# Attention steps that open with all their small matmuls, and gate weights sent once, in a two-block transformer kernel on one core

## The chip, the core and the metric

The kernel runs on one core of a Trainium2 chip. The metric is the device time of one launch, in microseconds (us); the time before is the median of three runs. Five engines work side by side and meet through semaphores: PE (TensorE, the matmuls), ACT (ScalarE), DVE (VectorE), POOL (GpSimd) and SP (SyncE, which here only issues DMAs).

## The reference

Two transformer blocks run one after the other on a sequence of 512 tokens of width 1024; the first adds 16 meta tokens (so 528 columns). Cut to the parts that the change touches:

```python
# first block: u = rmsnorm(h); proj = u @ w_in, split into q_na, k_na, v_na, q_gl, k_gl, v_gl, g_gl, z_gl
o_na = neighbourhood_attention(q_na, k_na, v_na, rpb)   # 8 heads of 64, window 8 rows x 16 columns, and the meta tokens
la_f = log_sigmoid(z[..., :16] @ up_f + bias_f) / 16     # z_gl is 32 columns wide: 16 for each direction
la_b = log_sigmoid(z[..., 16:] @ up_b + bias_b) / 16
o_gl = gla_bidirectional(...)                            # gated linear attention, chunks of 64
h = h + rmsnorm(concat(o_na, o_gl) @ w_o) ; feed-forward with a convolution of width 3
# second block
q, k, v, qi, ki, wi, u, ga, gb = split(h @ w_in_2)
sel = top_k(sum_j wi_j * relu(qi_j . ki), 128)           # for each query, among the keys before it
s = q . k / 8 - slope * distance, over the selected keys ; p = softmax(s) ; out = p @ v
merged = sigmoid(ga) * (out @ w_attn_proj) + sigmoid(gb) * (conv(u) @ w_conv_proj) ; ...
```

## The kernel before

**Precision.** All data is float32. Every large product is made from halves rounded to the format that PE reads fast: a value x is hi(x) + lo(x), and hi·hi + lo·hi + hi·lo makes three matmuls of one (`product`). `uhi` and `ulo` are the halves of the first block's normed input, `xhi` and `xlo` those of the second's, `whi` and `wlo` those of a weight.

**Weights.** 226 units of 128 x 1024 (512 KB) come in the order in which PE uses them, by SP (`load_unit`), into a ring of four slots `raw`. ACT rounds each to `whi` (`hi_through`), then its low half `wlo` is made: by DVE for units 0 and 1 (`split_unit`), by POOL from unit 2 on. A semaphore `unit_split` counts the low halves, `unit_used` frees a slot.

**The order** is written by hand: each engine has its own function, in which its instructions stand in the order of execution. Nothing reorders them, so an engine that waits holds all that stands behind it.

**The start.** The unit of z (index 0) holds z's 32 columns four times, so that PSUM has z in four groups of 32 rows; the gates' second product (`gate_logits`) then takes hi and lo of z and of the up-projections in one matmul. PE warms up on a constant tile (`keep_running`), and then runs z (unit 0) and the first tile of q_gl (unit 1) together, k after k (`two_tiles`), each with three products; `ulo` of each k comes from DVE (`first_low`), which also adds the squares for the norm (`add_square`). The second q_gl tile follows in halves (`half_tile`, destination B).

**Neighbourhood attention.** A loop of 18 steps in PE's, ACT's and DVE's functions. In step st PE makes the scores of step st, the transposes of the softmaxed scores of step st-1 and the values of step st-2; scores lie in the PSUM banks of `B4` (called B), values in `G[:, 1]`. Between them stand *pieces*: quarters of the 16 mixed projection tiles (`piece`, 12 matmuls each, all in the bank pair `G[:, 0]`), with `NA_SHARE[st]` pieces for step st. A tile's first piece waits for the evacuation of the tile before it (`evac_done`), which DVE makes in `after_piece` after the tile's last piece. In step 13 the transposes also wait for `meta_s_read`, DVE's reading of the meta tokens' scores, and `values_by_token(3)` turns the last tile of vT.

**Second attention.** A loop of 19 steps of the same kind, with a softmax over up to 512 keys (`soft2` on DVE, `exp2` on ACT), selections by top-k on DVE in steps 0 to 7, and pieces of the gates' projections (`gate_piece`). The waits of the small matmuls are `s2_read` (scores: the banks have been read), `p2_done` (transposes: the exp is there), `pt2_done` (values: the transposed weights are copied), `rb_done` and `al_done` (each fourth step: the block before has been scaled and split). PE's order of a step before is

```python
if 1 <= st < 16: scores2(st)
for x in ps[0:2]: gate_piece(x)
if 1 <= st <= 16: transposes2(st - 1)
for x in ps[2:4]: gate_piece(x)
if 2 <= st <= 17: values2(st - 2)
if st >= 5 and st % 4 == 1: factors2(st // 4 - 1)
for x in ps[4:]: gate_piece(x)
```

with 4 or 5 pieces in the steps 0 to 7 and two in the steps 8 to 15.

## Time and profile before

| | |
|---|---|
| median of three runs | 1465.36 us (1464.08 to 1465.66) |
| the profiled execution: its time | 1464.7 us |
| its span | 1462.8 us |
| busy in it: PE, DVE, ACT, POOL | 1435.7, 808.8, 557.6, 540.6 us |
| start, to the first half tile of B | 0 to 21.8 us |
| neighbourhood attention | 147.5 to 260 us |
| second attention | 868 to 1000 us |

A row of an engine in order of time gives the start, the duration, the engine and line, the operation with its destination and sources, its shape, the number of instructions, and in brackets the idle time ahead of it with what ended it. Consecutive instructions of one kind can share a row. Matmuls overlap, so the end of a record can lie past the start of the next; the distance between two starts says what an instruction costs PE.

### The profile page before, as it was taken

The numbers are of one execution on the slowest core, as the hardware profiler recorded it, in microseconds if no ns is written. First come the engines' busy times: TensorE is split into PE (matmuls) and PEld (weight loads), VectorE is DVE, ScalarE is ACT, GpSimd is POOL, SyncE is SP. The second block draws the span as 40 slices with busy tenths as digits, with TensorE's granted clock in tenths as the row PEclk, the third lists the DMA queues.
The fourth block names the chain that finished last, engine by engine and source line by source line (L and its number), as shares of the span: only waits on it lengthen the run. The fifth ranks groups of instructions, "written<-read, shape, count | busy, mean of one in ns | idle before, by whom it ended". The sixth has DMA issues, their size and how long they took to land.

```text
span 1462.8 us, 21184 instructions
## 1 busy us (share of the span) xinstructions
PE 1435.7 (98%) x8908; PEld 1238.4 (85%) x8908; DVE 808.8 (55%) x1154; ACT 557.6 (38%) x879; POOL 540.6 (37%) x229
## 2 busy tenths in 40 slices
PE   9999999999999999999999999999999999999997
PEld 8989787999999999888788767678888888888887
DVE  6933545446666666455799789863353344332023
ACT  6532334453223233232522464455344333333221
POOL 3421111224434434444244323224434444544441
PEclk9999999999999999999999999999999999999999
DMA  7211221112322224886232212212223233323332
GB/s 256 92 48 43 71 71 44 58 58 89 100 87 98 90 88 152 296 283 233 87 100 92 87 58 87 73 44 87 88 85 129 101 130 111 130 90 101 102 114 87
DMA packets 44830, 155.16 MB, mean 106 GB/s; under 512 B 4992, under 2 KB 7680, under 8 KB 44736
## 3 DMA queue, kind: packets, MB, share of 16 engines
q1 hardware_dynamic: 44080, 151.19, 31.1%
q10 hardware_dynamic: 656, 2.62, 0.6%
q8 instruction: 71, 1.16, 0.3%
q14 instruction: 23, 0.19, 0.0%
HBM read 151.56 MB, written 2.10 MB: 105 GB/s over the span
## 4 chain that ended last, share of the span: by engine, by line
PE 76%; DVE 6%; ACT 1%; issue 1%; DVEq 0%; ACTq 0%
PE G L512 71%; DVE scb L2259 1%; DVE small L2257 1%; PE B L1069 1%; PE B L1093 1%; PE B L1041 1%; DVE G L1759 1%; PE G L1080 0%; PE B L482 0%; DVE xlo L1767 0%; DVE S L2310 0%; DVE B L2306 0%; PE G L783 0%; DVE G L2200 0%; DVE small L2313 0%
## 5 line engine op out<-in xcount | busy, mean ns | idle before, releaser
L437 POOL TENSOR_TENSOR wlo<-raw,whi 128x1024 fp32r<-128x1024 f32 x224 | 540.1, 2413 | 900.5 <-ACT whi L1185 900.4
L1185 ACT ACTIVATE whi<-raw 128x1024 fp32r<-128x1024 f32 x226 | 238.5, 1056 | 292.7 <-DMA raw<-wstream 182.3
L512 PE MATMUL G<-xhi,whi 128*128 128x512 f32 (+1 forms) x692 | 273.5, 395 | 2.0 <-DVE xlo L1767 1.8
L512 PE MATMUL G<-xhi,wlo 128*128 128x512 f32 (+1 forms) x692 | 267.3, 386 | 0.0
L512 PE MATMUL G<-xlo,whi 128*128 128x512 f32 (+1 forms) x692 | 267.0, 386 | 0.0
L512 PE MATMUL G<-uhi,whi 128*128 128x258 f32 (+2 forms) x1216 | 253.3, 288 | 8.2 <-DVE qna L1901 1.7
L512 PE MATMUL G<-ulo,whi 128*128 128x258 f32 (+2 forms) x1216 | 246.3, 283 | 0.0
L512 PE MATMUL G<-uhi,wlo 128*128 128x258 f32 (+2 forms) x1216 | 245.8, 282 | 0.0
L512 PEld LDWEIGHTS G<-uhi,whi 128*128 128x128 f32 x1216 | 187.9, 189 | 21.1 <-issue 14.5
L512 PEld LDWEIGHTS G<-ulo,whi 128*128 128x128 f32 x1216 | 188.2, 189 | 0.0
L512 PEld LDWEIGHTS G<-uhi,wlo 128*128 128x128 f32 x1216 | 188.1, 189 | 0.0
L512 PEld LDWEIGHTS G<-xhi,whi 128*128 128x128 f32 x692 | 129.9, 188 | 44.7 <-issue 15.0
L512 PEld LDWEIGHTS G<-xhi,wlo 128*128 128x128 f32 x692 | 129.9, 188 | 26.7
L512 PEld LDWEIGHTS G<-xlo,whi 128*128 128x128 f32 x692 | 130.0, 188 | 24.7
L512 PE MATMUL G<-yhi,whi 128*128 128x512 f32 (+1 forms) x396 | 145.4, 367 | 0.0
L512 PE MATMUL G<-yhi,wlo 128*128 128x512 f32 (+1 forms) x396 | 144.8, 366 | 0.0
L512 PE MATMUL G<-ylo,whi 128*128 128x512 f32 (+1 forms) x396 | 144.7, 365 | 0.0
L2132 DVE TENSOR_TENSOR yf<-tv,tg 128x512 f32<-128x512 f32 x22 | 27.9, 1268 | 130.3 <-ACT tg L1273 130.3
L512 PEld LDWEIGHTS G<-yhi,wlo 128*128 128x128 f32 x396 | 74.7, 189 | 12.1
L512 PEld LDWEIGHTS G<-ylo,whi 128*128 128x128 f32 x396 | 74.7, 189 | 12.0
L512 PEld LDWEIGHTS G<-yhi,whi 128*128 128x128 f32 x396 | 74.7, 189 | 12.0
L2231 DVE SCALAR_TENSOR_TENSOR B<-z,vec,B 128x512 f32<-128x512 f32 x116 | 80.0, 751 | 1.1
(342 smaller groups left out, 1669.9 us busy)
## 6 DMA issues: line engine op xcount, KB each, us to landing
raw<-wstream SPq DMA_DIRECT2D x226, 512.0 KB, 3.4
ada_in<-ada SPq DMA_DIRECT2D x40, 512.0 KB, 5.8
ada_late<-ada SPq DMA_DIRECT2D x8, 512.0 KB, 3.6
h<-hT SPq DMA_DIRECT2D x8, 264.0 KB, 3.8
out<-res SPq DMA_DIRECT2D x8, 256.0 KB, 2.5
biasn<-bias SPq DMA_DIRECT2D x2, 960.0 KB, 7.5
biasn<-bias ACTq DMA_DIRECT2D x2, 960.0 KB, 4.7
scan_keep<-scanm SPq DMA_DIRECT2D x1, 528.0 KB, 6.8
```

The costliest lines, as they stand in the source:

```text
L437: pool.tensor_tensor(wlo[:, i, :], raw[:, i, :], whi[:, i, :].bitcast(F32), ALU.subtract)\
L512: ins = pe.matmul(dst[:, x, 0:xw], w[:, slot, b * P:(b + 1) * P], u[:, k, off + x0:off + x0 + xw], start=(first and i == 0 and j == 0), st ...
L1041: pe.matmul(B4[:, e % 4, 0:P * (b + 1)], qi2[par * 64:(par + 1) * 64, j // 2, P * b:P * (b + 1)], ki2[par * 64:(par + 1) * 64, 0:P * (b + ...
L1069: last = pe.matmul(B4[:, par, 0:P * (b + 1)], q2[par * 64:(par + 1) * 64, m, P * b:P * (b + 1)], k2[par * 64:(par + 1) * 64, m, 0:P * (b + ...
L1093: last = pe.matmul(B4[par * 64:(par + 1) * 64, 2 + b % 2, m * P:(m + 1) * P], v2[:, c, hh * 64:(hh + 1) * 64], pt2[r % 2][:, par, c * P:(c ...
L1185: act.activation(whi[:, m % RING, :], raw[:, m % RING, :], ACT.Copy).then_inc(s["unit_hi"], 1)
L1759: dve.scalar_tensor_tensor(normed_bank(i)[:, 0:w], h[:, k, META + c0:META + c0 + w], gain, B4[:, 2, c0:c0 + w], ALU.mult, ALU.mult).then_i ...
L2132: dve.tensor_tensor(y, value, tg[:, x, :], ALU.mult).then_inc(s["yf_done"], 1)
L2231: dve.scalar_tensor_tensor(B4[:, j, :], z, w, B4[:, j, :], ALU.mult, ALU.add).then_inc(s["tap_done"], 1)
L2257: link(dve.max(top8, x))
L2259: link(dve.match_replace(x, top8, x, TAKEN))
```

## The change

1. **z's weights.** Unit 0 is sent as 128 x 256 (z's columns once, `ZW` = 32 for each k). ACT rounds it into three groups of 32 columns, DVE writes its low half into the fourth (`split_z`). PE takes z in two passes, uhi and ulo, without wlo (`z_block`): 32 matmuls for 48, which wait for uhi and ulo apart; z of k+1 stands ahead of q_gl's product of k. The warm-up has 6 matmuls for 11. DVE splits units 2 and 3 also, POOL starts with unit 4; ACT's first square stands ahead of the rounding of unit 1, and SP sends unit 2 ahead of `vec` and unit 3 ahead of `scan_keep`. The low halves of z and of the up-projections are one group of rows.
2. **Neighbourhood attention.** In a step scores, transposes and values stand first, then all pieces. `NA_SHARE` now has tiles end with a step. ACT and DVE follow the same order.
3. **Second attention.** On PE scores, transposes and values stand ahead of all pieces. ACT, DVE and the number of pieces are as before.

```diff
-NA_SHARE = [3, 2, 3, 2, 3, 3, 2, 3, 2, 3, 3, 3, 2, 2, 0, 0, 0, 0]
+NA_SHARE = [4, 2, 2, 4, 2, 2, 4, 2, 2, 4, 2, 2, 2, 2, 0, 0, 0, 0]
...
-            load_unit(0)
+            sp.dma_start(raw[:, 0, 0:ZW * KD], wstream[0, :, 0:ZW * KD]).then_inc(s["unit_in0"], 16)
...
-            sp.dma_start(vec[:, KD:NVEC], vecs[:, KD:NVEC]).then_inc(s["vec_in"], 16)
...
             load_unit(2)
+            sp.dma_start(vec[:, KD:NVEC], vecs[:, KD:NVEC]).then_inc(s["vec_in"], 16)
             sp.dma_start(upt[:, :], up).then_inc(s["up_in"], 16)
+            load_unit(3)
             sp.dma_start(scan_keep[:, :, :], scanm).then_inc(s["gla_in"], 16)
-            load_unit(3)
...
-            for n in range(2, NUNIT):
+            for n in range(4, NUNIT):
...
-            keep_running(11, warm, warm)
+            keep_running(6, warm, warm)
...
-            two_tiles(U0["z"], T0["z"], lambda k: split_ready("mix_pre", k))
+            def z_block(k):
+
+                slot = U0["z"] % RING
+                for u, done in ((uhi, "uhi_done"), (ulo, "ulo_done")):
+                    pe.wait_ge(s[done], SPLITS["mix_pre"] + k + 1)
+                    for x in range(2):
+                        last = pe.matmul(G[:, T0["z"] % 2, x, 0:T // 2], whi[:, slot, k * P:(k + 1) * P],
+                                         u[:, k, x * (T // 2):(x + 1) * (T // 2)],
+                                         start=(k == 0 and u is uhi), stop=(k == KD - 1 and u is ulo))
...
+            unit_ready(U0["z"])
+            z_block(0)
+            unit_ready(U0["q_gl"])
+            for k in range(KD):
+                if k < KD - 1:
+                    z_block(k + 1)
+                last = product(G[:, T0["q_gl"] % 2], U0["q_gl"] % RING, [(k, k)], uhi, ulo, 0, T, first=(k == 0), last=(k == KD - 1))
...
                 if st < 16:
                     na_scores(st)
-                for x in ps[0:1]:
-                    piece(x)
                 if 1 <= st <= 16:
                     na_transposes(st - 1)
-                for x in ps[1:2]:
-                    piece(x)
                 if 2 <= st <= 17:
                     na_values(st - 2)
-                for x in ps[2:3]:
+                for x in ps:
                     piece(x)
...
                 if 1 <= st < 16:
                     scores2(st)
-                for x in ps[0:2]:
-                    gate_piece(x)
                 if 1 <= st <= 16:
                     transposes2(st - 1)
-                for x in ps[2:4]:
-                    gate_piece(x)
                 if 2 <= st <= 17:
                     values2(st - 2)
+                for x in ps[0:3]:
+                    gate_piece(x)
                 if st >= 5 and st % 4 == 1:
                     factors2(st // 4 - 1)
-                for x in ps[4:]:
+                for x in ps[3:]:
                     gate_piece(x)
...
-            hi_through(0)
+            act.wait_ge(s["unit_in0"], 16)
+            act.activation(whi[:, 0, :].rearrange("p (k g c) -> p k g c", g=4, c=ZW)[:, :, 0:3],
+                           raw[:, 0, 0:ZW * KD].rearrange("p (k c) -> p k c", c=ZW).unsqueeze(2).broadcast_to([P, KD, 3, ZW]),
+                           ACT.Copy).then_inc(s["unit_hi"], 1)
+            rounded[0] = 1
...
+                square("mix_pre", k, h[:, k, :])
                 if k == 0:
                     hi_through(1)
-                square("mix_pre", k, h[:, k, :])
...
+            def split_z():
+
+                high = whi[:, 0, :].rearrange("p (k g c) -> p k g c", g=4, c=ZW)
+                dve.wait_ge(s["unit_hi"], 1)
+                dve.tensor_tensor(high[:, :, 3], raw[:, 0, 0:ZW * KD].rearrange("p (k c) -> p k c", c=ZW),
+                                  high[:, :, 0].bitcast(F32), ALU.subtract).then_inc(s["unit_split"], 1)
...
-            split_unit(0)
+            split_z()
             first_low(0)
             split_unit(1)
             for k in range(1, KD):
                 first_low(k)
                 add_square("mix_pre", k)
+            split_unit(2)
             dve.wait_ge(s["act_step"], 2)
             dve.tensor_tensor(sum1[:, 1, :], rstd1[:, :], sum1[:, 0, :].bitcast(F32), ALU.subtract).then_inc(s["gate_low"], 1)
+            split_unit(3)
...
@@ ACT, neighbourhood attention
-                for x in ps[0:1]:
-                    after_piece(x)
                 if 1 <= st <= 16:
                     na_pt_evac(st - 1)
-                for x in ps[1:2]:
-                    after_piece(x)
                 if st < 16:
                     na_exp(st)
...
-                for x in ps[2:3]:
+                for x in ps:
                     after_piece(x)
...
@@ DVE, neighbourhood attention
                 if st < 16:
                     na_soft(st)
-                for x in ps[0:1]:
+                if 1 <= st <= 16 and st != 13:
+                    na_pt_copy(st - 1)
+                for x in ps if st != 13 else ():
                     after_piece(x)
...
-                if 1 <= st <= 16:
+                if st == 13:
                     na_pt_copy(st - 1)
-                for x in ps[1:3]:
-                    after_piece(x)
+                    for x in ps:
+                        after_piece(x)
```

PE at the start of the program, before: a row is one instruction or a run of alike ones, with destination, sources, columns and the semaphores that it waits for; `uhi,whi` is the first of a product's three parts.

```order
L446 MATMUL B<-warm 128x256 [waits warm_in]
L446 MATMUL B<-warm 128x256 x10
L512 MATMUL G<-uhi,whi 128x264 [waits ulo_done,unit_split]
L512 MATMUL G<-uhi,whi 128x264
L512 MATMUL G<-ulo,whi 128x264 x2
L512 MATMUL G<-uhi,wlo 128x264 x2
L512 MATMUL G<-uhi,whi 128x264 [waits unit_split]
```

PE at the same place, after:

```order
L447 MATMUL B<-warm 128x256 [waits warm_in]
L447 MATMUL B<-warm 128x256 x5
L567 MATMUL G<-uhi,whi 128x264 [waits uhi_done,unit_split]
L567 MATMUL G<-uhi,whi 128x264
L567 MATMUL G<-ulo,whi 128x264 [waits ulo_done]
...
L567 MATMUL G<-uhi,whi 128x264 [waits uhi_done,unit_split]
...
L513 MATMUL G<-uhi,whi 128x264 x2
L513 MATMUL G<-ulo,whi 128x264 x2
L513 MATMUL G<-uhi,wlo 128x264 x2
```

z's part with `wlo` is gone, and z of k = 0 and k = 1 stands ahead of the first product of q_gl, each half with its own wait.

PE in step 13 of the neighbourhood attention, before (L829 meta scores, L744 scores, L512 pieces, L761 transposes, L783 values, L793 factors, L729 the turn of vT):

```order
L829 MATMUL B<-kna,qna 16x16 [waits na_pt1,na_pt0]
L744 MATMUL B<-kna,qna 128x400 [waits na_s]
L512 MATMUL G<-uhi,whi 128x272
...
L761 MATMUL B<-ident,sc 128x128 [waits meta_s_read,vna_done,na_p,na_pt1,na_pt0]
...
L512 MATMUL G<-uhi,wlo 128x256
L783 MATMUL G<-pt,vna 64x128 [waits na_pt1,na_pt0,vna_done]
L793 MATMUL G<-ident,rbn 128x128 [waits na_div,na_rinv]
L729 MATMUL B<-ident,vT 128x128 [waits evac_done,na_pt1,na_pt0]
```

The same, after (L845, L764, L781, L803, L513, L813 and L749 are those lines now):

```order
L845 MATMUL B<-kna,qna 16x16 [waits na_pt1,na_pt0]
L764 MATMUL B<-kna,qna 128x400 [waits na_s]
L781 MATMUL B<-ident,sc 128x128 [waits meta_s_read,vna_done,na_p,na_pt1,na_pt0]
...
L803 MATMUL G<-pt,vna 64x128 [waits na_pt1,na_pt0,vna_done]
L513 MATMUL G<-uhi,whi 128x272
...
L513 MATMUL G<-uhi,wlo 128x256
L813 MATMUL G<-ident,rbn 128x128 [waits na_div,na_rinv]
L749 MATMUL B<-ident,vT 128x128 [waits evac_done,na_pt1,na_pt0]
```

The transposes that wait for `meta_s_read` now follow the scores directly, and the turn of vT, which waits for a tile's evacuation, has that tile's last pieces close ahead of it.

PE in step 9 of the second attention, before (L1069 scores, L1080 transposes, L1093 values, L1103 factors, L512 pieces):

```order
L1069 MATMUL B<-k__143,q__142 128x384 [waits s2_read]
L1069 MATMUL B<-k__143,q__142 128x384
L512 MATMUL G<-xhi,whi 128x512
...
L1080 MATMUL G<-ident,S_157 128x128 [waits pt2_done,p2_done]
L1080 MATMUL G<-ident,S_157 128x128 x2
L1093 MATMUL B<-pt2b,v__146 64x128 [waits pt2_done]
L1103 MATMUL B<-ident,rbc 128x128 [waits al_done,rinv2]
```

The same, after:

```order
L1085 MATMUL B<-k__143,q__142 128x384 [waits s2_read]
L1085 MATMUL B<-k__143,q__142 128x384
L1096 MATMUL G<-ident,S_157 128x128 [waits pt2_done,p2_done]
L1096 MATMUL G<-ident,S_157 128x128 x2
L1109 MATMUL B<-pt2b,v__146 64x128 [waits pt2_done]
L513 MATMUL G<-xhi,whi 128x512
...
L1119 MATMUL B<-ident,rbc 128x128 [waits al_done,rinv2]
```

The two pieces have moved from between the scores and the transposes to a place behind the values.

## Rows read from the trace of the kernel before

**Rows 1.** The page: busy time of PE, its share, instructions.
```profile
PE 1435.7 (98%) x8908; PEld 1238.4 (85%) x8908; DVE 808.8 (55%) x1154; ACT 557.6 (38%) x879; POOL 540.6 (37%) x229
```

**Rows 2.** Order of time, PE, start: start us, us, operation, [idle before].
```profile
1.10 7.37 PE L446 MATMUL B<-warm 128*128 128x256 f32 x22 [1.10 <-POOL warm L432]
...
5.09 0.63 PE L446 MATMUL B<-warm 128*128 128x256 f32 x1
...
5.52 0.57 PE L446 MATMUL B<-warm 128*128 128x256 f32 x1
...
10.45 0.51 PE L512 MATMUL G<-uhi,whi 128*128 128x264 f32 x2 [1.25 <-DVE wlo L1794]
...
21.82 0.51 PE L512 MATMUL B<-uhi,whi 128*128 128x264 f32 x2 [0.30 <-POOL wlo L437]
...
47.38 0.48 PE L512 MATMUL G<-uhi,whi 128*128 128x264 f32 x2 [0.75 <-DVE kgl L1817]
```

**Rows 3.** Order of time, ACT and DVE, start.
```profile
8.08 1.06 ACT L1185 ACTIVATE whi<-raw 128x1024 fp32r<-128x1024 f32 x1 [1.44 <-DMA raw<-wstream]
...
10.33 0.77 DVE L1799 SCALAR_TENSOR_TENSOR ulo<-h,vec,uhi 128x528 fp32r<-128x528 f32 x1
...
18.13 0.76 DVE L1799 SCALAR_TENSOR_TENSOR ulo<-h,vec,uhi 128x528 fp32r<-128x528 f32 x1
18.81 0.70 DVE L1789 TENSOR_TENSOR rstd<-rstd,sq 128x528 f32<-128x528 f32 x1
```

**Rows 4.** Stretches: PE, PEld, DVE, ACT, POOL busy, granted clock, DMA share, GB/s.
```profile
3.00:4.00 1.00, 1.00 (x4) 0.82 (x3) 0.00 (x0) 0.00 (x0) 0.00 (x0) 1.00 0.97 358
```

**Rows 5.** PE's waits, 147.5 to 249 us: total us, times, longest.
```profile
PE G L512 <- DVE qna L1901: 1.4, 2, 1.0
PE B L744 <- DVE kna L1901: 1.3, 1, 1.3
PE G L512 <- DVE vT L1901: 1.2, 2, 1.0
PE G L512 <- DVE kna L1901: 1.1, 2, 0.8
```

**Rows 6.** Order of time, PE, neighbourhood attention: a turn with and without wait.
```profile
156.08 0.27 PE L763 MATMUL B<-ident,sc 128*16 128x128 f32 x1
157.32 0.48 PE L512 MATMUL G<-uhi,whi 128*128 128x272 f32 x2 [0.96 <-DVE qna L1901]
...
162.16 0.27 PE L763 MATMUL B<-ident,sc 128*16 128x128 f32 x1
162.19 0.49 PE L512 MATMUL G<-uhi,whi 128*128 128x272 f32 x2
```

**Rows 7.** Order of time, PE and DVE, step 13 of neighbourhood attention.
```profile
243.92 0.41 PE L761 MATMUL B<-ident,sc 128*128 128x128 f32 x2 [0.83 <-DVE msc L2029]
...
246.35 1.11 DVE L1901 TENSOR_TENSOR vT<-G,rstd 128x512 f32<-128x512 f32 x1
```

**Rows 8.** Order of time, PE, DVE and ACT, second attention, steps 8 and 9.
```profile
943.77 0.92 PE L1069 MATMUL B<-k__143,q__142 64*128 64x384 f32 x4 [1.58 <-DVE S L2310]
...
947.52 0.82 PE L1080 MATMUL G<-ident,S 128*128 128x128 f32 x6
...
943.75 0.95 DVE L2313 TENSOR_REDUCE small<-S 128x2 f32<-128x768 f32 x1
...
945.86 0.19 ACT L1641 ACTIVATION_READ_ACCUMULATOR S<-S,small 128x1 f32 x1
```

**Rows 9.** Order of time, PE, ACT and DVE, second attention, steps 13 to 15.
```profile
972.46 0.59 ACT L1273 ACTIVATE sgb<-G 128x512 f32<-128x512 f32 x1
...
977.76 1.22 DVE L2313 TENSOR_REDUCE small<-S 128x2 f32<-128x1024 f32 x1
...
977.78 1.13 PE L1069 MATMUL B<-k__143,q__142 64*128 64x512 f32 x4
...
981.71 1.03 PE L1080 MATMUL G<-ident,S 128*128 128x128 f32 x8
```

More of the change, by code:

```diff
@@ L24 @@
 RANK = 16
+ZW = 2 * RANK
 DFF = 2816
@@ L578, in gate_logits @@
                     pe.wait_ge(s["ln_done"], 1)
-                    pe.wait_ge(s["gate_low"], 4)
+                    pe.wait_ge(s["gate_low"], 3)
                 elif j == 1:
@@ L1303, in gate_log @@
                 if j >= 2:
-                    act.wait_ge(s["gate_low"], 4 + j - 1)
+                    act.wait_ge(s["gate_low"], 3 + j - 1)
                 act.wait_ge(s["gate_x"], j + 1)
@@ L1808, in _ @@
                 add_square("mix_pre", k)
+            split_unit(2)
             dve.wait_ge(s["act_step"], 2)
             dve.tensor_tensor(sum1[:, 1, :], rstd1[:, :], sum1[:, 0, :].bitcast(F32), ALU.subtract).then_inc(s["gate_low"], 1)
+            split_unit(3)
             dve.wait_ge(s["act_step"], 3)
-            for rows in (slice(32, 64), slice(96, 128)):
-                dve.tensor_tensor(ups[rows, :], upt[rows, :], ups[rows, :].bitcast(F32), ALU.subtract).then_inc(s["gate_low"], 1)
+            dve.tensor_tensor(ups[32:64, :], upt[32:64, :], ups[32:64, :].bitcast(F32), ALU.subtract).then_inc(s["gate_low"], 1)
             def normed(dst, bank, rows=P):
@@ L2463, in layout @@
     r = lambda a, n=None: range(o[a], o[a + 1])
-    stream = _columns(w1, list(r(7)) * 4) + _columns(w1, r(3)) + _columns(w1, r(4)) + _columns(w1, r(5))
+    z = np.zeros((P, KD * P), np.float32)
+    z[:, :KD * ZW] = w1[:, list(r(7))].reshape(KD, P, ZW).transpose(1, 0, 2).reshape(P, KD * ZW)
+    stream = [z] + _columns(w1, r(3)) + _columns(w1, r(4)) + _columns(w1, r(5))
     part = {"q": 0, "k": 1, "v": 2, "g": 6}
```

9 lines of the change are left out of this document (6 added, 3 removed).

## The prediction, made before the changed kernel ran

> **What bounds the kernel now.** I read the page first: TensorE (PE) is busy 1435.7 us, 98% of the span [rows 1], so no transfer and no other engine sets the time; it is the sum of PE's matmuls and of the few places where PE stands still. An edit is worth what it does to those places, and it costs whatever new place it opens. I then read PE's order of time at the start of the program, PE's waits in the neighbourhood attention (147.5 to 249 us), and the order of time of the second attention (868 to 1000 us), with ACT and DVE beside it. The profiled execution took 1464.7 us, 0.66 under the median of the runs, 1465.36. I make the sum on the 1464.7 and add 0.66 at the end. What a measurement of this kernel can tell from no change is about 0.2%, or 2.9 us.
>
> **Part 1, z's weights.** In the kernel before, PE warms up to 8.47 and starts dense work at 10.45, after 1.25 us of waiting for DVE's low half of unit 1 [rows 2]. ACT could round unit 1 only at 8.08, having waited for its DMA for 1.44 us; ulo(1) stands at 10.33 to 11.10, so from that rounding to ulo(1)'s end 3.0 us pass [rows 3].
> - The DMA: unit 0 shrinks from 512 to 128 KB. The queue moves 358 GB/s at that time [rows 4], so 384 KB are 1.07 us, and unit 1 is rounded at about 7.0 and ulo(1) is there at 10.0. The rounding and splitting of z are no row of the trace; both lie before unit 1 on ACT and DVE, and are bounded by nothing and the 1.23-us class of a full unit. I take them as hidden, because both engines stand idle for the DMA there. If that cover is missing, up to 1.0 us of the gain goes.
> - The matmuls: 16 of z's 48 go. They ran at 16 products in some 11 us, 0.69 each, so z's third pass is about 8 x 0.23 = 1.8 us of PE. It is not the path: after the change PE needs 0.48 (z) + 0.72 = 1.20 us per k, and DVE delivers an ulo each 1.30 us, since seven of them (10.33 to 18.13) stand six steps apart [rows 3]. So ulo(7) ends at 10.0 + 6 x 1.30 = 17.8, after it PE has 0.24 (z's low pass) and two products of 0.72: 19.5.
> - The next tile: unit 2 goes to DVE. DVE's last add of a square (0.70 at 18.81) now ends at 18.4, the split takes 1.2, so PE goes on at 19.65 instead of 21.82 [rows 2, 3]: -2.1. Splits of units 2 and 3 add 2.5 us to DVE and leave POOL; unit 2's is on the path just counted, unit 3's is covered by the 4 us of half tile that PE still has. vec and scan_keep pass units 2 and 3 on SP's queue; their readers come after the half tiles, so I cost that at nothing. If one is late it meets the wait below.
> - Further on PE waits 0.75 us at 47.38 for DVE's kgl [rows 2], behind a chain of scans, part of which starts from DMA-bound units. It moves forward by all of 2.1 or by only 1.0 to 1.7. I take **-2.0**; bounds -3.2 (all of z's third pass and the full DMA gain) and +1.0 (nothing earlier, and z's split on the path).
>
> **Part 2, neighbourhood attention.** Pieces are quarters of projection tiles; a tile's evacuation must be done before the next tile's first piece overwrites its bank. PE waits there for qna, vT and kna: 1.4 + 1.2 + 1.1 us, in six places [rows 5]; their six records sum to 3.57. With tiles that end with a step, scores, transposes and values stand between the tile's last piece and the next tile's first one, 2.4 us or more, and all six vanish. The recorded waits are too small: a record ends up to 0.24 after the next start. At 156.08 a transpose is followed by the product at 157.32, 1.24 later; where nothing is awaited the same pair stands 0.03 apart (162.16 to 162.19) [rows 6]. So 1.21 is lost where 0.96 is recorded; six places so counted give **-4.36**.
> What comes in their place, in step 13: transposes(12) wait for the meta scores that DVE reads. Before, two pieces of 1.47 stand ahead, and 0.83 is still waited (0.97 by starts) [rows 7]. After, no piece stands there; the reader's time is unchanged, and 2.5 are waited: +1.55. In the same step the transposes of vT wait for an evacuation of 1.11 us at 246.35 that the last pieces hid [rows 7]; now it follows all pieces and only the factors (0.5) cover it: +0.95. The wait of scores for kna at step 12, 1.3 us [rows 5], stays. Going between products and the small matmuls costs up to 0.1 per turn by start-to-start distances; before a step has five or six turns, after four, but two small groups next to each other cost 0.05 to 0.09 too. Counted over the steps: about +0.25. DVE's evacuation now waits for the step's end behind na_soft and the copy of pt; ACT and DVE then have the three groups of the next step as cover. Sum -4.36 + 1.55 + 0.95 + 0.25 = **-1.6**; bounds -3.2 (step 13 adds 0.8 only) and +0.5 (two of six waits come back at 1 us).
>
> **Part 3, second attention.** Nothing is added, only PE's order changes: the two pieces that stood between scores(st) and transposes(st-1) now stand after values(st-2). In steps 0 to 8 DVE's selects pace PE, and the order matters little. From step 9 PE has no wait at all before, so everything that it must wait for is new.
> - Step 9: scores at 943.77 after a wait of 1.58 (kept, since DVE sets it), so PE asks for transposes(8) at 944.7. They need exp(8): DVE's maximum ends at 944.70, ACT's second exp at 946.05. Before, two pieces stood there and the transposes came at 947.52 [rows 8]. After, PE stalls 946.05 - 944.7 = **1.35**.
> - Step 15: transposes(14) hang on the chain evacuation of step 13 (972.46), rounding, rb, the scaling, three softmax operations of 3.7 us, the last ending at 978.98 [rows 9], and an exp like the 1.35 above: 8.2 to 8.5 long once step 13's pieces come first, against PE's cover of factors 0.6, transposes 1.0, values 1.0, scores with two pieces 3.93 (977.78 to 981.71 [rows 9]) and the next scores 1.06 = 7.6: **0.85**.
> - Values(12) wait for rb 0.2, transposes(10) 0.2, joins 0.4 (as in part 2); 0.3 comes back where DVE paces. Sum 1.35 + 0.85 + 0.2 + 0.2 + 0.4 - 0.3 = **+2.7**; bounds +0.5 (step 9's stall covered by an earlier start) and +4.
>
> **Sum.** -2.0 - 1.6 + 2.7 = -0.9 us: 1464.7 becomes 1463.8, on the median's basis **1464.4**.
>
> **The rivals.**
> - *Joins inside a step cost nothing, and step 13 stays as it was.* If small matmuls of different kinds follow without loss, 28 steps save two turns of 0.07, -3.9 us: 1460.5. The pair 162.16 to 162.19 [rows 6] speaks for it, the waits of step 13 [rows 7] against. Chance 0.18.
> - *PE's clock falls back in the thin stretch.* Between the end of the shorter warm-up (12 records, about 6.3) and 10.0 PE has only eight short matmuls. At the very start records stand 0.43 apart (5.09 to 5.52), and 22 of them end at 8.47, so the last dozen took half that each [rows 2]: about 4.4 us at half rate after the start. If that happened again at 10.0, two steps of k would take 2.4 instead of 1.3 us: +2.1, so the front gains nothing, 1466.5. Against it: after the idle time of 1.25 at 10.45 products run at 0.69 each, their full pace, and the PE of after does short work in between. The granted clock does not settle it, since it reads 1.00 from 3 to 4 us too [rows 4], where records stand 0.43 apart. Chance 0.15. The Trainium skill, "TensorE: Matmul & The Clock Gate", Part 1, "What's actually happening", speaks for this rival: an idle array returns from 2.4 to 1.2 GHz. By that rule the time would be the 1466.5; no row of before shows such a fall after a wait.
> - *The softmax chain is longer than PE's cover in every late step (the slower side).* At 512 keys the chain of scores, three DVE operations (1.2 to 1.3 each, as the reduction at 977.76 [rows 9]) and exp is about 5.3, PE's cover between a step's scores and its transposes 5.75 (scores and two pieces 3.93 of it [rows 9], transposes and values 0.8 to 1.0 each). It decides once the chain passes 5.75, as it does if DVE's other operations or ACT's rounding of 1.06 us come first. Then eight steps stall some 1.1 us, 8.8 instead of 2.35: +6.4, so 1470.8. For it: step 9 stalls by the row [rows 8]. Against: the margin of 0.45. Chance 0.12.
> - *Unit 1 does not come forward* (queue start-up, not bytes, sets its landing): the front gains 1.0 instead of 2.0, 1465.4. The queue ran at 358 GB/s in the window [rows 4], which speaks against it. Chance 0.03.
> - The forecast itself: 0.52, with a range of its own of 1462.5 to 1466.
>
> **How the numbers follow.** Faster than 1462.4: the first rival and some 0.08 of the forecast, 0.26. Slower than 1468.3: the third rival and 0.02 of the second, 0.14. Within: 0.60. The range of 8 in 10 reaches to 1460.3 (half of the first rival lies beyond) and to 1468.0 (most of the third does).
>
> **What would show it.** Right: dense PE work of the kernel after begins near 10.0, the half tile of B near 19.7; none of the waits for qna, kna, vT before a first piece is left in the neighbourhood attention, a wait of 2.5 for the meta scores and one near 1 for vT stand in step 13; in the second attention a wait of some 1.3 for exp(8) before transposes(8) and one under 1 before transposes(14). Wrong: products at twice their spacing, or a granted clock under 1, after 10 us, stalls in each late step, or waits for ACT or DVE before transposes and values of the neighbourhood attention.

## The result: slower by 0.2%, with TensorE's clock lowered for parts of the run

The changed kernel takes 1469.29 us (median of ten runs, 1465.91 to 1471.17) where the kernel before takes 1466.0 beside it: ratio 1.0021, 95% interval 1.0012 to 1.0029. The prediction said 1464.4 with a range to 1468.0; the time is outside of it and on the other side: a gain of 0.9 us was forecast, the loss is 3.3. The profiled execution of the changed kernel took 1468.1 us, 3.4 more than that of the kernel before.

The page of the changed kernel, its first rows: PE is busy 2.4 us longer than in [rows 1], with 26 records fewer.

```profile
span 1466.3 us, 21132 instructions
...
PE 1438.1 (98%) x8882; PEld 1239.5 (85%) x8882; DVE 806.5 (55%) x1155; ACT 559.5 (38%) x879; POOL 535.0 (36%) x227
```

I set the starts of the same PE instructions in both traces beside each other (after minus before). This shows where the time went:

| place | start, after minus before |
|---|---|
| 25 to 45 us | -1.0 us |
| 60 to 140 us | -1.1 |
| first turn of vT (146.76 before, 147.17 after) | +0.4 |
| scores of step 13 (240.48 before, 237.59 after) | -2.9 |
| turn of vT in step 13 (247.62 before, 248.82 after) | +1.2 |
| 262 to 868 us | +1.2 to +1.1 |
| behind the second attention (998.52 before, 1002.10 after) | +3.6 |
| end | +3.5 |

So there are two jumps that no edit explains by itself: 1.5 us between 140 and 147, where nothing was changed, and 4.1 us in step 13, where 2.5 were forecast. The view of stretches of the changed kernel (columns: PE, PEld, DVE, ACT, POOL busy, granted clock, DMA share, GB/s) shows what these places have in common.

```profile
10.80:14.00 3.20, 3.20 (x16) 3.20 (x16) 3.20 (x6) 3.20 (x6) 0.00 (x0) 0.50 0.75 222
...
140.50:143.70 3.20, 3.20 (x16) 3.20 (x15) 0.06 (x1) 2.16 (x4) 0.96 (x1) 0.50 0.00 0
...
242.90:246.10 3.20, 3.20 (x15) 3.20 (x16) 0.00 (x0) 1.54 (x4) 1.78 (x1) 0.50 0.00 0
```

The same stretches of time in the kernel before:

```profile
10.80:14.00 3.20, 3.20 (x29) 3.20 (x28) 3.20 (x6) 3.20 (x7) 0.00 (x0) 1.00 0.90 290
...
140.50:143.70 3.20, 3.20 (x27) 3.13 (x26) 0.30 (x2) 3.17 (x6) 0.00 (x0) 1.00 0.00 0
```

In three stretches the granted clock is 0.50, 1.2 GHz, and PE gets through 15 or 16 records in 3.2 us where it otherwise has 27 to 29. PE counts as fully busy there, which is why its busy time rose. Step 13 shows how such a stretch comes about (PE in order of time, the changed kernel; columns as in [rows 2]).

```profile
237.59 0.94 PE L764 MATMUL B<-kna,qna 64*128 64x400 f32 x4
241.03 0.41 PE L781 MATMUL B<-ident,sc 128*128 128x128 f32 x2 [2.50 <-DVE msc L2053]
...
243.35 0.65 PE L513 MATMUL G<-ulo,whi 128*128 128x272 f32 x2
243.80 0.64 PE L513 MATMUL G<-uhi,wlo 128*128 128x272 f32 x2
...
246.59 0.41 PE L513 MATMUL G<-uhi,whi 128*128 128x272 f32 x2
246.84 0.40 PE L513 MATMUL G<-ulo,whi 128*128 128x272 f32 x2
...
248.82 0.63 PE L749 MATMUL B<-ident,vT 128*128 128x128 f32 x4 [0.90 <-DVE vT L1923]
```

The wait for the meta scores is 2.50, as forecast, and that for vT 0.90. But behind the first one products stand 0.45 apart (243.35, 243.80) until 246, then 0.25 (246.59, 246.84). The two pieces, from 242.76 to 247.32, take 4.56 us where two pieces of 1.47 are 2.94: 1.6 us lost to the clock. At the start it is the same: PE waits 2.26 for unit 1, and then z and q_gl run at twice their spacing (0.44 from 11.18 to 11.62, 0.24 from 14.44 to 14.68).

```profile
9.70 0.52 PE L567 MATMUL G<-uhi,whi 128*128 128x264 f32 x2 [2.26 <-DVE wlo L1808]
...
11.18 0.64 PE L513 MATMUL G<-ulo,whi 128*128 128x264 f32 x2
11.62 0.64 PE L513 MATMUL G<-uhi,wlo 128*128 128x264 f32 x2
...
14.44 0.41 PE L567 MATMUL G<-ulo,whi 128*128 128x264 f32 x2
14.68 0.41 PE L513 MATMUL G<-uhi,whi 128*128 128x264 f32 x2
```

The second attention came out as forecast in kind: a wait for exp(8) in step 9 and a small one before transposes(14), both absent in [rows 8, 9].

```profile
944.80 0.92 PE L1085 MATMUL B<-k__143,q__142 64*128 64x384 f32 x4 [1.34 <-DVE S L2334]
946.53 1.15 PE L1096 MATMUL G<-ident,S 128*128 128x128 f32 x6 [0.81 <-ACT S L1655]
...
982.16 1.36 PE L1096 MATMUL G<-ident,S 128*128 128x128 f32 x8 [0.21 <-ACT S L1655]
```

### The profile page after: what moved, and what is told of

The parts are those of the page before. It is cut to its first block, busy times and chain, and to the rows that moved or that the text cites. A ratio compares the mean times of both kernels' runs of the same rounds, so it can differ in the third digit from the quotient of the medians.

```text
span 1466.3 us, 21132 instructions
## 1 busy us (share of the span) xinstructions
PE 1438.1 (98%) x8882; PEld 1239.5 (85%) x8882; DVE 806.5 (55%) x1155; ACT 559.5 (38%) x879; POOL 535.0 (36%) x227
## 4 chain that ended last, share of the span: by engine, by line
PE 76%; DVE 6%; ACT 2%; issue 1%; DVEq 0%; ACTq 0%
PE G L513 72%; DVE scb L2283 1%; DVE small L2281 1%; PE B L1057 1%; DVE G L1773 1%; PE B L1109 0%; DVE S L2334 0%; PE B L1085 0%; DVE B L2330 0%; DVE small L2337 0%; PE B L483 0%; PE G L1096 0%; DVE xlo L1781 0%; PE G L803 0%; DVE G L2224 0%
## 5 line engine op out<-in xcount | busy, mean ns | idle before, releaser
L438 POOL TENSOR_TENSOR wlo<-raw,whi 128x1024 fp32r<-128x1024 f32 x222 | 534.5, 2409 | 908.4 <-ACT whi L1199 908.4
L513 PE MATMUL G<-xhi,whi 128*128 128x512 f32 (+1 forms) x692 | 272.8, 394 | 2.0 <-DVE xlo L1781 1.8
L513 PE MATMUL G<-xhi,wlo 128*128 128x512 f32 (+1 forms) x692 | 267.3, 386 | 0.0
L513 PE MATMUL G<-xlo,whi 128*128 128x512 f32 (+1 forms) x692 | 267.2, 386 | 0.0
L513 PE MATMUL G<-uhi,whi 128*128 128x258 f32 (+3 forms) x1200 | 250.1, 289 | 3.2 <-DVE sg L1839 0.9
L513 PE MATMUL G<-uhi,wlo 128*128 128x258 f32 (+3 forms) x1200 | 244.9, 285 | 0.0
L513 PE MATMUL G<-ulo,whi 128*128 128x258 f32 (+3 forms) x1200 | 244.1, 284 | 0.0
L513 PEld LDWEIGHTS G<-uhi,whi 128*128 128x128 f32 x1200 | 187.3, 191 | 9.7 <-issue 7.2
L513 PEld LDWEIGHTS G<-uhi,wlo 128*128 128x128 f32 x1200 | 187.3, 191 | 0.0
L513 PEld LDWEIGHTS G<-ulo,whi 128*128 128x128 f32 x1200 | 187.0, 191 | 0.0
L513 PEld LDWEIGHTS G<-xhi,whi 128*128 128x128 f32 x692 | 129.9, 188 | 40.1 <-issue 10.5
L513 PEld LDWEIGHTS G<-xhi,wlo 128*128 128x128 f32 x692 | 130.0, 188 | 26.8
L513 PEld LDWEIGHTS G<-xlo,whi 128*128 128x128 f32 x692 | 130.1, 188 | 24.7
L513 PE MATMUL G<-yhi,whi 128*128 128x512 f32 (+1 forms) x396 | 145.5, 367 | 0.0
L513 PE MATMUL G<-yhi,wlo 128*128 128x512 f32 (+1 forms) x396 | 144.9, 366 | 0.0
L513 PE MATMUL G<-ylo,whi 128*128 128x512 f32 (+1 forms) x396 | 144.9, 366 | 0.0
L513 PEld LDWEIGHTS G<-yhi,whi 128*128 128x128 f32 x396 | 74.8, 189 | 12.0
L513 PEld LDWEIGHTS G<-ylo,whi 128*128 128x128 f32 x396 | 74.8, 189 | 12.0
L513 PEld LDWEIGHTS G<-yhi,wlo 128*128 128x128 f32 x396 | 74.7, 189 | 11.9
```

Source lines behind the costliest of these rows:

```text
L438: pool.tensor_tensor(wlo[:, i, :], raw[:, i, :], whi[:, i, :].bitcast(F32), ALU.subtract)\
L513: ins = pe.matmul(dst[:, x, 0:xw], w[:, slot, b * P:(b + 1) * P], u[:, k, off + x0:off + x0 + xw], start=(first and i == 0 and j == 0), st ...
```

## The experiments

The theory (the clock theory): the changed kernel loses because PE stands still or thins out for longer at one go, at the start and in step 13, and runs at half rate behind it. The rival (waits alone): the loss is made of the waits and turns in PE's order, and the clock adds nothing that the change brought. Each row below is a kernel, its median and that of the kernel before on the same chip (two chips were used, so rows are compared by their ratios), the ratio with its 95% interval, and the granted clock of all its runs, averaged (the profile gives it for the whole execution to three digits; a lower one means more time at half rate, wherever in the program).

| kernel | us | before | ratio (interval) | clock |
|---|---|---|---|---|
| changed kernel | 1469.29 | 1466.0 | 1.0021 (1.0012 to 1.0029) | 0.9941 |
| part 1 alone | 1464.22 | 1465.49 | 0.9995 (0.9986 to 1.0004) | 0.9965 |
| part 1, warm-up of 11 | 1463.14 | 1465.49 | 0.9991 (0.9982 to 1.0000) | 0.9976 |
| part 2 alone | 1467.48 | 1465.49 | 1.0014 (1.0005 to 1.0023) | 0.9959 |
| part 3 alone | 1468.28 | 1465.49 | 1.0020 (1.0011 to 1.0029) | 0.9975 |
| part 2, wait of step 13 filled | 1465.23 | 1465.65 | 0.9997 (0.9988 to 1.0006) | 0.9972 |
| part 2, step 13 mended | 1462.30 | 1465.65 | 0.9978 (0.9969 to 0.9987) | 0.9971 |
| part 3, step 9 mended | 1467.20 | 1465.65 | 1.0011 (1.0002 to 1.0020) | 0.9975 |
| before, step 13 reordered | 1471.06 | 1465.21 | 1.0042 (1.0030 to 1.0055) | 0.9962 |
| changed kernel, filled | 1466.91 | 1465.21 | 1.0011 (1.0003 to 1.0020) | 0.9969 |
| parts 1 and 2, both mended | 1459.71 | 1465.65 | 0.9961 (0.9948 to 0.9974) | 0.9976 |
| the same, two more waits filled | 1459.61 | 1465.21 | 0.9963 (0.9949 to 0.9976) | 0.9982 |

The kernel before itself has 0.998 on average (32, 27 and 15 runs gave 0.9980, 0.9978 and 0.9979; single runs 0.995 to 0.999). Not all that is missing to 1 is lost time: in each of the thirteen profiles the clock is 0.50 in the last 2.8 to 5.8 us as well, behind PE's last matmul, where it costs nothing. In the kernel before, whose last matmul ends at 1455.9:

```profile
1460.00:1462.80 2.80, 0.00 (x0) 0.00 (x0) 0.22 (x1) 0.00 (x0) 0.00 (x0) 0.50 0.70 231
```

The three profiles without any other such stretch read 0.998 or 0.999, those with one 0.997 or 0.998, those with three or four 0.995 or 0.994. So it is the runs at 0.997 and lower that tell of a stretch inside the program. The kernel before has 29 of them in 74, though not in its profiled one, and they take 1466.35 us on average where its 27 runs at 0.999 take 1464.66.

### The parts one by one

Part 1 alone, all its hunks of the diff and none of the others:

```diff
+ZW = 2 * RANK
...
-            keep_running(11, warm, warm)
+            keep_running(6, warm, warm)
```

> The kernel before with part 1 alone (z's weights, warm-up of 6). Clock theory: PE's products from 10.7 to 14.1 us run at twice their spacing again, the half tile of B starts near 20.9 (21.8 before), the rest of the program is 1.1 us early: 1464.3 where the kernel before is 1465.4, less if a further stretch at half rate (about 1.6 us each) falls into the run. Rival, the order of DVE sets the start and the clock does not matter: the same 1.1, but without a stretch at a granted clock of 0.5 in the profile.

The same with the longer warm-up:

```diff
+ZW = 2 * RANK
...
             keep_running(11, warm, warm)
```

> Part 1 alone, with the warm-up of 11 matmuls kept, so that PE works until 8.5 us where it otherwise thins out from 6.6. Clock theory: no stretch at half rate at 10 us, products 0.24 per pair from the first, the half tile of B near 19.7, the program 2.0 us early instead of 1.1. Rival (DVE's low halves set the start): 20.9 and 1.1 as with the short warm-up.

The first row is part 1 with the short warm-up, the second with the long one (stretches, columns as above):

```profile
9.80:12.90 3.10, 3.01 (x14) 2.86 (x14) 3.10 (x6) 3.10 (x7) 0.00 (x0) 0.50 0.88 258
```
```profile
9.80:12.90 3.10, 3.10 (x24) 3.03 (x25) 3.10 (x6) 3.10 (x6) 0.00 (x0) 1.00 0.88 260
```

In the profiles the clock theory holds: 14 records at a clock of 0.50 against 24 at 1.00, the half tile of B starts at 20.4 and at 19.3 (20.9 and 19.7 were expected), and the instruction that starts at 25 us in the kernel before starts 1.5 us earlier with the short warm-up and 2.5 earlier with the long one. One pair of profiles would not do for this, since the old start by itself puts that instruction anywhere from 1.1 early to 1.3 late in its profiles; but all four kernels with the new start and the long warm-up have it 2.5 to 2.9 early, both with the short one 1.0 and 1.5. So the first rival, that DVE alone sets the start, is out. Of that gain, at 50 us, 0.2 and 1.7 are left: the wait for kgl (0.75 in [rows 2]) is 1.4 in both, and the short version has a second one of 0.4. The size of the gain is decided at that wait, which my expectation of 1.1 and 2.0 did not have. Of the times, 1464.2 and 1463.1, the two intervals overlap; they don't tell the versions apart by themselves.

Part 2 alone:

```diff
-NA_SHARE = [3, 2, 3, 2, 3, 3, 2, 3, 2, 3, 3, 3, 2, 2, 0, 0, 0, 0]
+NA_SHARE = [4, 2, 2, 4, 2, 2, 4, 2, 2, 4, 2, 2, 2, 2, 0, 0, 0, 0]
```

> Part 2 alone. Between the first scores and the first pieces after the loop: steps 0 to 12 gain 3.3 us, step 13 loses 2.5 by its waits. Clock theory: after the 2.5 us wait in step 13 the granted clock is 0.5 for some microseconds and costs 1.6 more, in sum +0.8 us. Rival (waits alone): the granted clock stays at 1.00 in step 13, in sum -0.8 us.

The profiled execution had two such stretches in a row behind the wait, and lost 5.7 us in step 13 (3.3 us were gained in steps 0 to 12). PE in order of time, then the stretches:

```profile
242.54 0.41 PE L761 MATMUL B<-ident,sc 128*128 128x128 f32 x2 [2.59 <-DVE msc L2023]
```
```profile
239.00:243.00 4.00, 1.41 (x12) 0.77 (x9) 2.71 (x5) 0.00 (x0) 0.00 (x0) 1.00 0.00 0
243.20:246.40 3.20, 3.20 (x20) 2.32 (x19) 0.56 (x1) 2.75 (x7) 0.57 (x1) 0.50 0.00 0
246.60:249.80 3.20, 3.20 (x16) 3.20 (x16) 0.00 (x0) 0.00 (x0) 1.60 (x1) 0.50 0.00 0
```

The sum is +2.0 us, more than the 0.8 expected with one stretch and far from the -0.8 of the rival.

Part 3 alone is the hunk of the second attention in the diff:

```diff
-                for x in ps[0:2]:
-                    gate_piece(x)
                 if 1 <= st <= 16:
                     transposes2(st - 1)
...
+                for x in ps[0:3]:
+                    gate_piece(x)
```

> Part 3 alone. Both theories: +2.5 us, of which 1.15 in step 9 (transposes wait for the exp), 0.2 in each of the steps 10 to 12 by joins, 0.5 to 0.8 behind step 14. The clock theory adds that no wait is over 0.9 us there, so the granted clock stays at 1.00 between 868 and 1000 us. Rival of the prediction (each late step stalls): +6.4.

+2.8 us, where 2.5 were expected, but the profile does not show it all by the steps that I gave: in it the second attention is 3.7 longer than before, since here, too, a stretch at half rate follows the two waits of step 9, against what the clock theory said of waits that short.

```profile
943.66 0.92 PE L1069 MATMUL B<-k__143,q__142 64*128 64x384 f32 x4 [1.35 <-DVE S L2308]
945.39 1.54 PE L1080 MATMUL G<-ident,S 128*128 128x128 f32 x6 [0.81 <-ACT S L1639]
```
```profile
945.40:948.60 3.20, 3.20 (x16) 2.34 (x17) 2.16 (x4) 2.46 (x7) 0.00 (x0) 0.50 0.01 3
```

This stretch can't be put down to the new order. With the old order in step 9, where PE waits 1.58 for the scores, three of eight profiles have one there too (part 1 with the long warm-up, part 2 with the fill, and the reordered kernel before, 1.55 us each), with the new order one of three. The row is part 2 with the fill:

```profile
943.20:946.40 3.20, 3.20 (x9) 2.42 (x9) 2.80 (x4) 1.18 (x4) 0.00 (x0) 0.50 0.01 3
```

The mean clock of part 3, 0.9975, is near that of the kernel before; so its cost is mainly one of waits and turns.

### The wait and the clock taken apart

Part 2 with five matmuls of no use in the wait of step 13. They don't shorten the wait, they only keep PE working:

```diff
                 if st < 16:
                     na_scores(st)
+                if st == 13:
+                    pe.wait_ge(s["na_div"], 2)
+                    for _i in range(5):
+                        pe.matmul(G[:, 1, 1, 0:256], ones[:, 0:P], vec[:, 0:256], start=True, stop=True)
                 if 1 <= st <= 16:
                     na_transposes(st - 1)
```

> Part 2 alone, with five matmuls of 256 columns into an unused bank between scores(13) and transposes(12): the wait for the meta scores stays as long as it is (2.5 us), but PE works through most of it. Clock theory: the granted clock stays at 1.00 in step 13, the stage gains 3.3 and loses 2.5, in all 1464.6 where the kernel before is 1465.4 and part 2 alone was 1467.4; mean granted clock up from 0.9959 to about 0.998. Rival (waits alone): the wait costs what it costs, 1467.4 as part 2 alone.

PE in order of time, and the stretches that follow:

```profile
236.29 0.94 PE L744 MATMUL B<-kna,qna 64*128 64x400 f32 x4
237.16 2.43 PE L813 MATMUL G<-vec,ones 128*128 128x256 f32 x10
239.73 0.41 PE L761 MATMUL B<-ident,sc 128*128 128x128 f32 x2
```
```profile
237.00:242.00 5.00, 4.85 (x34) 3.54 (x33) 3.27 (x6) 1.71 (x6) 0.00 (x0) 1.00 0.00 0
242.00:246.00 4.00, 3.13 (x26) 2.89 (x25) 1.16 (x2) 1.14 (x2) 2.38 (x1) 1.00 0.09 24
```

From the scores to the transposes 3.44 us pass, as without the fill (3.44 in the changed kernel, 237.59 to 241.03; 3.53 in part 2 alone). The clock stays at 1.00, and the kernel takes 1465.2 instead of 1467.5. The two intervals of the ratio, 0.9988 to 1.0006 and 1.0005 to 1.0023, hardly touch. This is the cleanest test of the study: the same waits, the same useful work, 0.17% apart. The traces agree: step 13 loses 2.6 us in both kernels with the fill, which is its waits, and 4.1 to 5.7 in the three that wait as long without one. Waits alone are out.

The other way round: the kernel before with nothing changed but the place of two pieces in step 13.

```diff
-                for x in ps[0:1]:
+                for x in ps[0:1] if st != 13 else ():
                     piece(x)
                 if 1 <= st <= 16:
                     na_transposes(st - 1)
-                for x in ps[1:2]:
+                for x in ps[1:2] if st != 13 else ():
                     piece(x)
                 if 2 <= st <= 17:
                     na_values(st - 2)
-                for x in ps[2:3]:
+                for x in ps[2:3] if st != 13 else ps:
                     piece(x)
```

> The kernel before with one edit: in step 13 of the neighbourhood attention the two pieces stand behind transposes and values. Two waits grow, by 1.55 and 0.95 us. Clock theory: the wait of 2.5 us is followed by one or two stretches at half rate in most runs, so the loss is 2.5 + 1.6 to 3.2 = 4.1 to 5.7 us (1469.8 to 1471.3), mean granted clock about 0.0015 lower. Rival (waits alone): 2.5 us, 1468.1, clock as before.

```profile
246.19 0.41 PE L761 MATMUL B<-ident,sc 128*128 128x128 f32 x2 [2.50 <-DVE msc L2029]
```
```profile
248.20:251.20 3.00, 3.00 (x15) 3.00 (x15) 0.00 (x0) 1.40 (x5) 2.38 (x1) 0.50 0.00 0
```

One step of one loop, +5.9 us. In the trace 4.1 us are lost between step 13's start and 262 us, 2.5 by the two waits and 1.6 by the stretch. Where the rest of the 5.9 is, the one trace does not show: it has further stretches at half rate at 142 and 951 us, places that the edit doesn't touch, and how often such ones come in the runs without a profile is only seen in the mean clock, 0.9962 against 0.9979.

The changed kernel with the fill and the longer warm-up:

```diff
-            keep_running(6, warm, warm)
+            keep_running(11, warm, warm)
...
+                if st == 13:
+                    pe.wait_ge(s["na_div"], 2)
+                    for _i in range(5):
+                        pe.matmul(G[:, 1, 1, 0:256], ones[:, 0:P], vec[:, 0:256], start=True, stop=True)
```

> The changed kernel whole, with the warm-up of 11 and with five matmuls of 256 columns in the wait of step 13. No wait is shorter and no work is left out. Clock theory: the two places where the granted clock fell most often are covered, mean granted clock 0.997 where the changed kernel had 0.994; time 1.8 (start) + 0.3 (neighbourhood attention with the fill) under and 2.9 (second attention) over the kernel before: 1466.4, where the changed kernel is 3.4 over it. Rival (waits and turns alone): the fill changes nothing, only the longer warm-up does, 1468.

1466.9, that is 1.7 over the kernel before instead of 3.3: some half of what the change lost is taken back by matmuls that compute nothing. What is left is less than part 3 alone had cost. Neither the start nor step 13 has a stretch at half rate in its profile, but a place that no edit touches has one, at 710 us (see the last section).

### Mending the order

Part 2 with the pieces of step 13 ahead of its transposes:

```diff
                 if st < 16:
                     na_scores(st)
+                for x in ps if st == 13 else ():
+                    piece(x)
                 if 1 <= st <= 16:
                     na_transposes(st - 1)
                 if 2 <= st <= 17:
                     na_values(st - 2)
-                for x in ps:
+                for x in ps if st != 13 else ():
                     piece(x)
```

> Part 2 alone, but in step 13 the two pieces stand ahead of the transposes. Both theories: neither the wait of 2.5 us for the meta scores nor that of 0.9 for vT is left. Clock theory: no stretch at half rate in step 13 either, in all 3.9 to 4.5 us under the kernel before (1461.2). Rival (waits alone): 2.5 us under part 2 alone, 1465.0.

PE's waits of this kernel, 232 to 262 us (columns as in [rows 5]): the wait for the meta scores [rows 7] is gone, as are the six evacuations of [rows 5] earlier on; kna of step 12 is still there, the waits for pt and mpt are those of the kernel before, and 0.3 is left of the one for vT.

```profile
PE B L744 <- DVE kna L1895: 1.3, 1, 1.3
PE G L783 <- DVE pt L1981: 0.9, 1, 0.9
PE B L761 <- ACT mpt L1444: 0.3, 1, 0.3
PE B L729 <- DVE vT L1895: 0.3, 1, 0.3
```

3.4 us under the kernel before, 1462.3 (the clock theory had 1461.2, the rival 1465.0); part 2 with one exception is a gain. Its profile has no stretch at half rate in step 13, but one at 142 us.

Part 3 with the pieces of step 9 ahead of its transposes:

```diff
+                for x in ps if st == 9 else ():
+                    gate_piece(x)
                 if 1 <= st <= 16:
                     transposes2(st - 1)
                 if 2 <= st <= 17:
                     values2(st - 2)
-                for x in ps[0:3]:
+                for x in ps[0:3] if st != 9 else ():
                     gate_piece(x)
```

> Part 3 alone, but in step 9 the two pieces stand ahead of the transposes. Theory (the exp in step 9 and joins): of the 2.9 us that part 3 cost, 1.15 go; 0.2 in each of steps 10 to 12 and the stall behind step 14 stay: +1.7 against the kernel before, 1467.1. Rival (the chain of steps 9 to 16 is late as a whole, and a gain in step 9 is lost again behind it): +2.9 as before.

The time, 1467.2, is the one expected, but the trace gives the point to the rival:

```profile
949.79 0.66 PE L1103 MATMUL B<-ident,rbc 128*128 128x128 f32 x4
...
951.23 0.88 PE L1080 MATMUL G<-ident,S 128*128 128x128 f32 x6
953.06 0.88 PE L1093 MATMUL B<-pt2a,v__146 128*64 128x128 f32 x12 [0.96 <-issue]
```

The stall before transposes(8) is gone, but values(8) now stand still for 0.96 us. By the program they wait for rb, which ACT copies after the factors of step 9 (949.79), and no piece lies between; the profile names no releaser. From the scores of step 9 to the first product behind the loop 57.0 us pass (944.76 to 1001.77), 57.3 in the changed kernel (944.80 to 1002.10) and 54.75 in the kernel before (943.77 to 998.52), so only 0.3 is won. The rest of the difference in time to part 3 lies within both intervals.

The two gains together, with the second attention as it was:

```diff
             keep_running(11, warm, warm)
...
+                for x in ps if st == 13 else ():
+                    piece(x)
```

> Part 1 with the warm-up of 11, part 2 with the pieces of step 13 ahead of its transposes, the second attention as in the kernel before. If the parts add: 1.8 + 4.1 = 5.9 us under the kernel before, 1459.5. Rival (the gain of the start is lost in the neighbourhood attention, where DVE and ACT then set the pace): 1461.3.

1459.71 us, ratio 0.9961 (0.9948 to 0.9974): the parts add, and this version beats both kernels. In its trace PE is 1.5 us ahead at 140 us and 5.3 ahead at 250.

The same with two more waits filled:

```diff
+                if st == 12:
+                    pe.wait_ge(s["na_div"], 2)
+                    for _i in range(3):
+                        pe.matmul(G[:, 1, 1, 0:256], ones[:, 0:P], vec[:, 0:256], start=True, stop=True)
...
+                if st == 9:
+                    pe.wait_ge(s["al_done"], 1)
+                    for _i in range(3):
+                        pe.matmul(B4[:, 2, 0:256], ones[:, 0:P], vec[:, 0:256], start=True, stop=True)
```

> The version with part 1 at a warm-up of 11, part 2 with step 13 mended and the old second attention, with three matmuls of 256 columns ahead of each of the two longest waits left (kna in step 12, 1.3 us; scores of step 9 of the second attention, 1.6 us). Clock theory: falls of the granted clock behind these two become rarer, the mean clock rises by up to 0.0005, the time falls by 0 to 0.7 us: 1459.2 to 1459.9. Rival (a wait under 1.6 us does not lower the clock): no difference, 1459.8, or up to 0.3 more where the fill outlasts the wait.

1459.61 against 1459.71, 0.9982 against 0.9976 in mean clock: no difference in time that could be told. Whether waits of 1.3 to 1.6 us cost the clock often enough to be worth a fill stays open.

## Why the prediction was wrong

**What failed: the clock rival was priced at one place only.** I saw that PE's clock could fall in a thin stretch, gave that 0.15, and looked for it at the start alone, where it came (products 0.44 apart from 10.7 to 14.1). But the sum of part 2 itself forecast a wait of 2.5 us in step 13, the longest in the program, and I carried it as 1.55 + 0.95 and nothing behind it. The argument against, that 1.25 us of idle at 10.45 had lowered nothing [rows 2], was drawn from one profiled execution. Its trace has a fall behind PE's work after all, at its end, where PE has nothing left to do (0.50 behind 1460). The kernel before does have stretches at half rate in other executions, as its clock of 0.997 and lower in 29 of 74 shows, and the same start, unchanged, had one in the profile of part 2 alone after 1.90 us of waiting (PE, and the stretch):

```profile
10.77 0.61 PE L512 MATMUL G<-uhi,whi 128*128 128x264 f32 x2 [1.90 <-DVE wlo L1786]
```
```profile
11.10:14.30 3.20, 3.20 (x17) 3.20 (x16) 3.20 (x6) 3.20 (x7) 0.00 (x0) 0.50 0.91 288
```

One trace can show that a fall is possible, not that it does not occur. Between the two profiles the difference is 3.5 us where -0.9 was forecast; of these 4.4 us, 1.6 are the stretch in step 13, 1.5 the one at 140 us, which is no part of the change, and 0.9 the gain of the start that did not come.

**Part 1, forecast -2.0.** In the profile of the changed kernel -1.1, by the time of part 1 alone about -0.8 to -1.3, with the long warm-up about -1.3 to -2.3. Right: unit 1 was rounded at 7.34 (7.0 forecast), and DVE delivers an ulo each 1.30; with the long warm-up PE keeps to that pace, so z in two passes is not the path. Wrong: the shorter warm-up, which I had named only in the rival; with it PE runs without a break from 10.38 and reaches the half tile of B at 20.92 where 19.65 were forecast. (A product takes 0.72, not the 0.69 of the prediction, which changes no term.) And PE's start behind the wait for kgl, to which I gave 1.0 to 1.7 of the gain to lose or keep, moves by itself by some 0.9 us either way between profiles of the same start code (see the last section), so a single profile couldn't settle it.

**Part 2, forecast -1.6.** Steps 0 to 12 gained 3.3 instead of 4.1: all six waits of [rows 5] went, but two new ones came, and the turns were mis-sized. In steps 6 and 10 the transposes, which now follow the scores directly, stand still for a moment: they start 0.69 and 0.66 behind the last scores, 0.43 elsewhere behind scores of that size. By the program they wait there for ACT's copy of the turned vT; the profile names no releaser. That is 0.5 of the 0.8 us. The turns make the rest, 0.55 where I had counted 0.25: products follow transposes after 0.03 [rows 6], but values follow them after 0.21. PE in the changed kernel, steps 2, 6 and 10:

```profile
161.30 0.27 PE L783 MATMUL B<-ident,sc 128*16 128x128 f32 x1
161.51 1.02 PE L803 MATMUL G<-pt,vna 128*64 128x128 f32 x12
...
188.24 0.52 PE L781 MATMUL B<-ident,sc 128*128 128x128 f32 x3 [0.19 <-issue]
...
218.91 0.52 PE L781 MATMUL B<-ident,sc 128*128 128x128 f32 x3 [0.16 <-issue]
```

Step 13's two waits were right to 0.05 (2.50 and 0.90); that two pieces stood ahead of its transposes was a slip, it is one, which changes no number. The term of the clock, 1.6 in the profile of the changed kernel and 3 in that of part 2 alone, was missing.

**Part 3, forecast +2.7.** 2.5 in the trace, 2.8 in time. Step 9 was right in sum: the first half of the transposes waits only for its own exp, so 0.88 by starts ahead of it and 0.3 within it, where I had 1.35 in one. The stall of transposes(14) is smaller, 0.3 ahead of them and 0.3 within, where I had 0.85. Instead turns and waits of 0.1 to 0.2 cost 0.2 a step here too (scores to scores 5.35 before, 5.57 after in step 10), 0.9 in all where I had 0.4. So the sum came out by errors that cancel. The rival in which every late step stalls did not come; its price did not follow from its own terms either (a chain of 5.3 + 1.06 against a cover of 5.75 is 0.6 a step, not 1.1).

**The sum.** Without the clock it would be -2.0 - 0.8 + 2.7, near 0; the changed kernel with fill and long warm-up, +1.7 with an interval from 0.4 to 2.9, comes towards that, with a clock still lower than the kernel before. The jump of 1.5 us at 140 us is no part of the change: PE has groups of matmuls with 16 columns there in both kernels, and the clock fell behind them in five of the twelve profiles other than that of the kernel before, in kernels whose edits lie elsewhere or later. That the mean clock of the changed kernel is the lowest of all, 0.9941, is shown, and the parts add up to it: they lie 0.0015, 0.0021 and 0.0005 under the 0.9980 beside them, which makes 0.9939. As an estimate, 0.0038 of 1466 us, the difference to the kernel before, is some 5.6 us of PE's work, less where PE stands still in such a stretch; that would be enough for the whole miss of 4.2 in the medians. Which share falls at which place in the runs without a profile is not shown.

The Trainium skill, "TensorE: Matmul & The Clock Gate", Part 1, "What's actually happening", says that an idle array returns to 1.2 GHz and adds that the point of transition differs from run to run. The traces agree on the first: 0.50 behind 2.5 to 2.6 us of waiting in three kernels. On the second they show that the same code may fall or not: at the start 1.00 in the profile of the kernel before, after 1.25 us of waiting, and 0.50 in that of part 2 alone, after 1.90.

## What to carry to other kernels

Where PE is the bound, count the longest single wait of an order, not only the sum of the waits: a wait of 2.5 us at one go cost 1.6 us more behind it, in one profile 3, while six waits of 0.2 to 1.0 cost only themselves. When an order takes cover away from a wait, first look for pieces that can stay ahead of just that wait (one step treated apart turned +2.0 us into -3.4); if there are none, matmuls that compute nothing hold the clock. And read the granted clock of several executions before a fall is ruled out by one, with the end of the program, where PE has finished, taken off.
